# First products on x times its weight ahead of each norm, and four modulation slabs summed beside layer 0's first attention

## The chip, the cores and the metric

One core of a Trainium2 chip runs the whole program. The metric is device time in microseconds, the median of three runs. TensorE multiplies (PE in the profile), VectorE is DVE, ScalarE is ACT, GpSimd is POOL, and SP's queue issues the loads of weights.

## The reference

A first block (RMS norm; three branches: forgetting attention, an S5 state space, memory attention; gated merge; output projection; residual) ends in an outer RMS norm. Two layers follow, on 512 tokens of 1024 features, each modulated by a vector c:

```
ada = silu(c) @ w_ada[l] + b_ada[l]          # shift, scale, gate; twice 3 x 1024
h   = rms(x, g_mix[l]) * (1 + sc1) + sh1
q, k, v of two attentions, gate_a, gate_b = split(h @ w_in[l])
x   = x + gt1 * ((sigmoid(gate_a) * y_a + sigmoid(gate_b) * y_b) @ w_out[l])
h2  = rms(x, g_mlp[l]) * (1 + sc2) + sh2
x   = x + gt2 * (relu(h2 @ w_ff1[l])**2 @ w_ff2[l])
```

`rms(x, g)` divides each token by the root of its mean square and multiplies by g. A product with h can also be made as rstd * (W^T (g (1 + sc) x)) + W^T sh, with rstd one number per token.

## The kernel before

x lies transposed in SBUF, features on partitions, eight blocks k of 128 features by 512 tokens. Each fp32 product is made of three fp32r products: high x high, high x low, low x high. So one tile (128 output features by 512 tokens) is 24 matmuls of 512 columns. Weights come in slabs of 256 columns (1 MB) into a ring of three slots, in one order written by `plan_slabs` (L275); SP issues a slab's load when the slab three before it is used up (`load_weights`, L185). GpSimd splits each slab into a high and a low part, half a slab at a time (L268 high, L272 low), into room for four halves; a half is free when the tile made of it is done. Stages are written out one after another, each engine's queue in program order, with waits on semaphores.

The modulation is 48 slabs, 24 a layer ("ada"). Each is loaded through the same ring, scaled by ScalarE (L395, eight instructions), summed by VectorE (L408), turned by TensorE (L422) and taken by VectorE (L431, L434). `tiles_stage` (L438) does this beside its tiles: scaling and sum two tiles ahead of a slab's last tile, turn and take three tiles later. Four of them lie in the first block's output stage and three in layer 0's.

`norm_stage` (L741) runs four times: at the outer norm and layer 0's mix norm together (`twice`), and at layer 0's MLP norm, layer 1's mix norm and layer 1's MLP norm. Sums of squares are turned by one-column matmuls (L779), then root, reciprocal and spreading transposes (L789); then for each block k VectorE scales (L867), ScalarE adds the shift and rounds (L841), VectorE makes the low part (L860). Matmuls on constants (`warm`, L785) stand in the waits, except in the double norm. Nothing is multiplied by h until h's first block is there.

In a layer the norm is followed by `qkv_stage` (six groups of 96 products), `turn_stage` (transposes), `attention_stage` (16 steps), `wide_attention_stage` (8 steps), mixing, output, the second norm and the MLP. The 16 gate tiles (384 products) are a `Stream` fed between the pieces of the turn and attention stages, by the numbers called paces: 72 by the end of the turn stage, to 252 in the attention stage at 9 a step, to 384 in the wide one at 14 a step. ScalarE takes each stream tile with a Tanh (L2736). The first block's output stage adds x by residue (L2426), squares it twice on ScalarE (L2438, L2440) and adds the squares on VectorE (L2423).

## Time and profile before

| | us |
|---|---|
| median of three runs | 2288.77 (2288.75 to 2291.99) |
| profiled execution | 2291.23 |
| its span | 2289.4 |
| TensorE busy | 2249.8 (98%) |
| GpSimd busy | 1691.9 (74%) |
| VectorE busy | 1259.3 (55%) |
| ScalarE busy | 632.8 (28%) |
| mean granted TensorE clock | 0.992 |

A matmul's record lasts longer than the time to the next one's start, since they are pipelined: read the spacing of starts, not the busy time. The busy time also covers the constants' matmuls and the one-column matmuls in a norm.

### The profile page before, as it was taken

How to read it: one execution, taken by the hardware profiler on the slowest of the kernel's cores; microseconds unless marked ns; L12 is line 12 of the kernel's file. 1: busy time of each engine (PE TensorE's matmuls, PEld its weight loads, DVE VectorE, ACT ScalarE, POOL GpSimd, SP SyncE). 2: the span in 40 equal slices, each digit the busy share in tenths (PEclk: the TensorE clock that was granted, in tenths of full speed). 3: DMA queues.
4: the chain of work that ended last, by engine and by line, in shares of the span. 5: the costliest groups of instructions: out<-in, count | busy, mean ns of one | idle time of the engine just before them, and what ended most of it. 6: DMA issues, size and time to landing. Idle time of an engine off the chain costs nothing.

```text
span 2289.4 us, 31094 instructions
## 1 busy us (share of the span) xinstructions
PE 2249.8 (98%) x11693; PEld 1828.1 (80%) x11693; DVE 1259.3 (55%) x1798; ACT 632.8 (28%) x1286; POOL 1691.9 (74%) x2678
## 2 busy tenths in 40 slices
PE   8999999999999999999999999999999999999999
...
GB/s 204 129 137 153 268 151 35 116 101 159 159 186 186 111 111 94 50 36 39 164 131 189 174 191 177 184 107 97 100 79 33 29 124 92 154 107 107 92 92 56
DMA packets 268656, 280.87 MB, mean 123 GB/s; under 512 B 29964, under 2 KB 240592, under 8 KB 268508
## 3 DMA queue, kind: packets, MB, share of 16 engines
...
## 4 chain that ended last, share of the span: by engine, by line
PE 85%; POOL 6%; DVE 4%; issue 2%; ACT 2%; DMA 1%; SPq 0%; ACTq 0%; DVEq 0%; POOLq 0%
PE ps L496 46%; PE ps L674 14%; PE ps L2527 4%; PE ps L2528 4%; PE ps L2529 4%; POOL ring_low L272 4%; POOL ring_high L268 3%; PE ps L982 2%; PE ps L1025 2%; PE ps L1001 2%; PE ps L1175 1%; PE ps L1182 1%; PE ps L1158 1%; PE ps L2637 1%; DVE ada_acc L408 1%
## 5 line engine op out<-in xcount | busy, mean ns | idle before, releaser
L272 POOL TENSOR_TENSOR ring_low<-ring,ring_high 128x256 fp32r<-128x256 f32 x1309 | 1039.0, 824 | 28.4
L268 POOL TENSOR_SCALAR ring_high<-ring 128x256 fp32r<-128x256 f32 x1309 | 609.1, 491 | 478.3 <-PE ps L674 170.8
L496 PE MATMUL ps<-hT_high,ring_high 128*128 128x512 f32 x704 | 278.0, 395 | 1.4 <-DVE hT_low L860 1.4
L496 PE MATMUL ps<-hT_low,ring_high 128*128 128x512 f32 x704 | 274.9, 390 | 0.0
L496 PE MATMUL ps<-hT_high,ring_low 128*128 128x512 f32 x704 | 274.0, 389 | 0.0
L674 PE MATMUL ps<-hT_high,ring_high 128*128 128x512 f32 x568 | 234.5, 413 | 3.2 <-POOL ring_low L272 1.4
L674 PE MATMUL ps<-hT_high,ring_low 128*128 128x512 f32 x568 | 225.3, 397 | 0.0
L674 PE MATMUL ps<-hT_low,ring_high 128*128 128x512 f32 x568 | 225.1, 396 | 0.0
L408 DVE TENSOR_REDUCE ada_acc<-ring 128x256 f32<-128x2048 f32 x48 | 188.8, 3933 | 54.8 <-ACT ring L395 54.7
L496 PE MATMUL ps<-hidden_high,ring_high 128*128 128x512 f32 x512 | 201.0, 393 | 0.0
L496 PE MATMUL ps<-hidden_low,ring_high 128*128 128x512 f32 x512 | 199.6, 390 | 0.0
L496 PE MATMUL ps<-hidden_high,ring_low 128*128 128x512 f32 x512 | 199.3, 389 | 0.0
L395 ACT ACTIVATE ring<-ring,c_act 128x256 f32<-128x256 f32 x384 | 158.4, 499 | 81.7 <-DMA ring<-in_w_ada_dram 71.4
L2902 DVE SCALAR_TENSOR_TENSOR xT<-ps,ada,xT 128x512 f32<-128x512 f32 x64 | 48.0, 751 | 233.0 <-PE ps L496 233.0
L496 PEld LDWEIGHTS ps<-hT_high,ring_high 128*128 128x128 f32 x704 | 132.1, 188 | 32.1 <-DVE hT_low L860 2.9
L496 PEld LDWEIGHTS ps<-hT_high,ring_low 128*128 128x128 f32 x704 | 132.3, 188 | 28.3
L496 PEld LDWEIGHTS ps<-hT_low,ring_high 128*128 128x128 f32 x704 | 132.3, 188 | 26.0
L2527 PE MATMUL ps<-ring_high,hT_high 128*128 128x512 f32 x384 | 150.6, 392 | 2.1 <-DVE hT_low L860 2.1
L2528 PE MATMUL ps<-ring_high,hT_low 128*128 128x512 f32 x384 | 150.4, 392 | 0.0
L2529 PE MATMUL ps<-ring_low,hT_high 128*128 128x512 f32 x384 | 150.2, 391 | 0.0
L674 PEld LDWEIGHTS ps<-hT_high,ring_high 128*128 128x128 f32 x568 | 106.8, 188 | 40.3 <-issue 17.9
L2943 ACT ACTIVATE relu<-ps 128x512 f32<-128x512 f32 x64 | 38.2, 599 | 347.7 <-PE ps L496 341.8
...
## 6 DMA issues: line engine op xcount, KB each, us to landing
ring<-in_w_in_dram SPq DMA_DIRECT2D x75, 1024.0 KB, 5.3
ring<-in_w_ff_dram SPq DMA_DIRECT2D x64, 1024.0 KB, 5.4
ring<-in_w_ada_dram SPq DMA_DIRECT2D x48, 1024.0 KB, 5.4
ring<-in_w_out_dram SPq DMA_DIRECT2D x12, 1024.0 KB, 5.8
...
ring<-in_w_mem_kv_dram SPq DMA_DIRECT2D x4, 1024.0 KB, 5.4
...
```

The lines of the kernel that those rows point to most:

```text
L268: ins = nc.gpsimd.tensor_scalar(x(hi), x(raw), 1.0, 1.0, ALU.mult, ALU.mult)
L272: ins = nc.gpsimd.tensor_tensor(x(lo), x(raw), x(hi).bitcast(F32), ALU.subtract)
L395: ins = K.nc.scalar.activation(w[:, k, :], w[:, k, :], ACT.Copy, scale=K.c_act[:, k:k + 1])
L408: K.nc.vector.tensor_reduce(K.ada_acc[:, n % 2, :], K.slot(slab).rearrange("p k n -> p n k"), AX_X, ALU.add).then_inc(K.sig("ada_scaled"). ...
L496: return nc.tensor.matmul(out[0:rows, bank, cols[0]:cols[1]], lhsT, rhs, start=start, stop=stop)
L674: ins = K.nc.tensor.matmul(out, lhsT, rhs, start=start, stop=stop)
L982: ins = nc.tensor.matmul(s_view(i, u, w)[:, c:c + n], lhsT, rhs, start=True, stop=st["diagonal"] is None or c + n < w)
L1001: ins = nc.tensor.transpose(t_view(u, w)[:, b * P:(b + 1) * P], probs[j % P_BUFS][:, u, b * P:(b + 1) * P], K.ident)
L2527: nc.tensor.matmul(out, xh, hi[:, y, :], start=k == 0, stop=False)
L2528: nc.tensor.matmul(out, xl, hi[:, y, :], start=False, stop=False)
L2529: ins = nc.tensor.matmul(out, xh, lo[:, y, :], start=False, stop=k == KD - 1)
L2902: return v.scalar_tensor_tensor(K.xT[:, m, :], ps[:, 0, :], gate[:, m:m + 1], K.xT[:, m, :], ALU.mult, ALU.add)
```

## The change

The two first gate tiles of each layer, and the first hidden tile of each MLP, are made on x times its weight g(1 + sc), without the root. Their two operands (high by ScalarE, low by VectorE) are made during the eight tiles ahead of the norm. In the norm, TensorE goes through the eight blocks k: the tiles' products, then two two-column matmuls a tile that multiply the shift by the same weights, with the turning and spreading of the root between blocks. VectorE scales the finished tiles by the root; the shift's product goes in as a bias of the Tanh or Relu. The normed h is written over the same two operands, each block after its products are done (`used`). The gate slab `m{l}0ga` so moves ahead of the qkv slabs. The stream has 14 tiles (336 products) with new paces. In the first norm of all and the MLP norms the scaled block lies in PSUM instead of SBUF.

One modulation slab leaves the first block's output stage and three leave layer 0's output stage: four are now done beside layer 0's first attention, a third of a slab's scaling and a third of its sum per step. The mixing stage no longer waits for the last stream tile before its fourth tile, and the first sums of squares in the first output stage move from ahead of the tile's addition into `ahead`.

```diff
     for i in range(4):
         add("out", T["w_out"][0], dm, 0, D, part=i)
-        ada(0)
+        if i < 3:
+            ada(0)
...
+        add(f"m{l}0ga", w2, dm, 3072, D, part=0)
...
         for mp in range(4):
-            add(f"m{l}{mp}ga", w2, dm, 3072, D, part=mp)
+            if mp:
+                add(f"m{l}{mp}ga", w2, dm, 3072, D, part=mp)
+                if l == 0 and mp > 1:
+                    ada(0)
             add(f"m{l}{mp}gb", w2, dm, 4096, D, part=mp)
+            if l == 0 and mp in (1, 2):
+                ada(0)
...
-            if l == 0 and i < 3:
-                ada(0)
...
+    def scale(self, e, i):
+        K = self.K
+        slab, r = self.due(i)
+        if slab is None:
+            return
+        if r == 0:
+            K.slab_here(e, slab)
+        w = K.slot(slab)
+        for k in range(3 * r, min(3 * r + 3, KD)):
+            ins = K.nc.scalar.activation(w[:, k, :], w[:, k, :], ACT.Copy, scale=K.c_act[:, k:k + 1])
+        if r == 2:
+            ins.then_inc(K.sig("ada_products").sem, 1)
+    def add(self, e, i):
+        K = self.K
+        slab, r = self.due(i - 3)
+        if slab is None:
+            return
+        l, x = K.ada_slab[slab]
+        n = l * 24 + x
+        if r == 0:
+            e.wait_ge(K.sig("ada_products").sem, n + 1)
+            e.wait_ge(K.sig("ada_summed").sem, n - 1)
+        cols = ((0, 86), (86, 171), (171, 256))[r]
+        ins = K.nc.vector.tensor_reduce(K.ada_acc[:, n % 2, cols[0]:cols[1]],
+                                        K.slot(slab)[:, :, cols[0]:cols[1]].rearrange("p k n -> p n k"), AX_X, ALU.add)
+        if r == 2:
+            ins.then_inc(K.sig("ada_scaled").sem, 1)
+    def sum(self, pe, j):
+        K = self.K
+        slab, r = self.due(j - 5)
+        if slab is None or r:
+            return
+        l, x = K.ada_slab[slab]
+        n = l * 24 + x
+        pe.wait_ge(K.sig("ada_scaled").sem, n + 1)
+        pe.wait_ge(K.sig("ada_taken").sem, n)
+        for c in range(2):
+            ins = K.nc.tensor.transpose(K.ps[:, 4, SLAB_W + c * P:SLAB_W + (c + 1) * P],
+                                        K.ada_acc[:, n % 2, c * P:(c + 1) * P], K.ident)
+        ins.then_inc(K.sig("ada_summed").sem, 1)
+    def take(self, e, j):
+        K = self.K
+        slab, r = self.due(j - 5)
+        if slab is None or r:
+            return
+        l, x = K.ada_slab[slab]
+        n = l * 24 + x
+        e.wait_ge(K.sig("ada_summed").sem, n + 1)
+        K.link(e, "dve_step", K.nc.vector.tensor_reduce(
+            K.ada_col[:, n % 2, :], K.ps[:, 4, SLAB_W:2 * SLAB_W].rearrange("p (c k) -> p c k", c=2), AX_X, ALU.add))
+        K.nc.vector.tensor_tensor(K.ada[:, l, 2 * x:2 * x + 2], K.ada_col[:, n % 2, :], K.b_ada[l][:, 2 * x:2 * x + 2], ALU.add
+                                  ).then_inc(K.sig("ada_taken").sem, 1)
 def tiles_stage(K, tiles, banks, act=None, dve=None, act_on=None, after=None, entry=None, arriving=None, tensor_entry=None, act_lead=4,
-                also=None, ahead=None, ada_bank=7, late=None, entry_at=None, waits=None, ada_lead=2, ada_lag=3, back=None):
+                also=None, ahead=None, ada_bank=7, late=None, entry_at=None, waits=None, ada_lead=2, ada_lag=3, back=None, done=0):
...
+                first = 2 + done
                 size = len(tiles[0])
...
-def norm_stage(K, src, gain, dst, shift, sums, last, twice=None, banks=(7, 6, 1)):
+def factors_ahead(K, e, shift):
...
+        self.high, self.low = K.sig("unnormed_high"), K.sig("unnormed_low")
+        self.base = self.high.total
+        self.high.total += KD
+        self.low.total += KD
+    def round_up(self, e, k):
+        K = self.K
+        K.nc.scalar.activation(K.hT[0][:, k, :], self.src[:, k, :], ACT.Copy, scale=self.gain[:, k:k + 1]
+                               ).then_inc(self.high.sem, 1)
+    def low_part(self, e, k):
+        K = self.K
+        e.wait_ge(self.high.sem, self.base + k + 1)
+        K.nc.vector.scalar_tensor_tensor(K.hT[1][:, k, :], self.src[:, k, :], self.gain[:, k:k + 1],
+                                         K.hT[0][:, k, :].bitcast(F32), ALU.mult, ALU.subtract).then_inc(self.low.sem, 1)
+def norm_stage(K, src, gain, dst, shift, sums, last, unnormed, tiles, places, made, take, twice=None):
...
+                pe.wait_ge(unnormed.low.sem, unnormed.base + k + 1)
+                for n, t in enumerate(tiles):
+                    if k == 0:
+                        K.weight_here(pe, t[0][5])
+                    for x in range(3 * k, 3 * k + 3):
+                        _, rows, cols, lhsT, rhs, _, start, stop = t[x]
+                        ins = nc.tensor.matmul(ps[0:rows, tile_banks[n], cols[0]:cols[1]], lhsT, rhs, start=start, stop=stop)
+                ins.then_inc(used.sem, 1)
+            def shift_of(n, k):
+                for x in (3 * k, 3 * k + 2):
+                    ins = nc.tensor.matmul(ps[:, shift_bank, 2 * n:2 * n + 2], tiles[n][x][3], K.shift_two[:, k, :],
+                                           start=x == 0, stop=x == 3 * KD - 1)
+                if (n, k) == (len(tiles) - 1, KD - 1):
+                    ins.then_inc(made.sem, len(tiles))
...
+            def turn(bank, parts):
+                for t in range(TT):
+                    for n, x in enumerate(parts):
+                        ins = nc.tensor.matmul(ps[:, bank, t:t + 1], x[:, t * P:(t + 1) * P], K.ones[:, 0:1],
+                                               start=n == 0, stop=n == len(parts) - 1)
+                ins.then_inc(turned.sem, 1)
...
+            pe.wait_ge(taken.sem, taken.total - 2)
+            for k in range(KD):
+                products_of(k)
+                if twice is not None:
+                    squared, summed = twice[0]
+                    for h in (2 * k, 2 * k + 1):
+                        shift_of(h // KD, h % KD)
+                    if k == 1:
+                        pe.wait_ge(taken.sem, taken.total)
+                        pe.wait_ge(summed.sem, summed.total)
+                        pe.wait_ge(squared.sem, squared.total - 1)
+                        turn(turn_bank, (sums, last))
+                    if k == 3:
+                        pe.wait_ge(inverted.sem, i0 + 1)
+                        spread_root(root_bank, 4)
+                    if k == 4:
+                        pe.wait_ge(squared.sem, squared.total)
+                        turn(other_bank, (twice[3], twice[4]))
+                    if k == 6:
+                        pe.wait_ge(inverted.sem, i0 + 2)
+                        spread_root(other_bank, 1)
+                else:
+                    for h in range(len(tiles) * k, len(tiles) * (k + 1)):
+                        shift_of(h // KD, h % KD)
+                    if k == (2 if len(tiles) == 1 else 1):
+                        pe.wait_ge(taken.sem, taken.total)
+                        turn(turn_bank, (sums, last))
+                    if k == (4 if len(tiles) == 1 else 2):
+                        pe.wait_ge(inverted.sem, i0 + 1)
+                        spread_root(root_bank, 4)
...
+                pe.wait_ge(copied.sem, c0 + 1)
...
+            unnormed.round_up(e, KD - 1)
...
-                nc.scalar.activation(dst[0][:, k, :], tmp[:, k % 2, :], ACT.Identity, bias=shift[:, k:k + 1]
+                e.wait_ge(used.sem, u0 + k + 1)
+                nc.scalar.activation(dst[0][:, k, :], tmp[k % 2], ACT.Identity, bias=shift[:, k:k + 1]
...
+                if k == 0 and twice is not None:
+                    e.wait_ge(root.sem, o0 + 2)
+                    v.reciprocal(nar[:, 1, :], nar[:, 0, :]).then_inc(inverted.sem, 1)
                 if k >= 1:
                     low_part(k - 1)
             low_part(KD - 1)
+            K.link(e, "dve_step", v.tensor_copy(rstd[:, :], ps[:, root_bank, :]))
+            e.wait_ge(made.sem, made0 + len(tiles))
+            for n in range(len(tiles)):
+                K.link(e, "dve_step", v.tensor_reduce(K.shift_of[:, n:n + 1], ps[:, shift_bank, 2 * n:2 * n + 2], AX_X, ALU.add))
+                take(e, n, ps[:, tile_banks[n], :], rstd[:, :])
...
+                    if beside is not None and len(beside) > 2:
+                        beside[2](pe, j)
...
-    tmp = R("normed0", [P, 2, SEQ], 57344)
+    tmp = [ps[:, b, :] for b in (0, 3)]
...
-                if k >= 2:
-                    e.wait_ge(by_act.sem, by_scalar.index(k) + 1)
-                v.scalar_tensor_tensor(tmp[:, k % 2, :], K.xT[:, k, :], K.g_norm[:, k:k + 1], ps[:, 1, :], ALU.mult,
+                if k >= 1:
+                    e.wait_ge(by_act.sem, by_scalar.index(max(k, 3)) + 1)
+                v.scalar_tensor_tensor(tmp[k % 2], K.xT[:, k, :], K.g_norm[:, k:k + 1], ps[:, 1, :], ALU.mult,
...
+        if n < KD - 1:
+            unnormed.round_up(e, n)
...
+    def first_gains(e, n):
+        if n == 0:
+            mix_gains(K, e, 0)
+        if n >= 2:
...
+        if n >= 1:
+            unnormed.low_part(e, n - 1)
...
-    summed.total += KD - 3
...
+    summed.total += KD - 2
...
+                if g == 1:
+                    pe.wait_ge(*gates_scaled)
...
+            e.wait_ge(*gates_turned)
...
+    K.link(e, "gains_ready", x)
+    factors_ahead(K, e, ada[:, 0:8])
...
+    def scale_gates(e, n, ps, rstd):
+        v.tensor_tensor(scaled_gates[n][:, :], ps, rstd, ALU.mult)
+        v.tensor_scalar(K.half_shift[:, n:n + 1], K.shift_of[:, n:n + 1], 0.5, None, ALU.mult).then_inc(gates_scaled.sem, 1)
...
+            if mp or b == "b":
+                tiles += column_tiles(K, K.first[f"m{l}{mp}g{b}"], 2, KD, K.hT)
...
+    def turn_gates(e):
+        e.wait_ge(gates_scaled.sem, gates_scaled.total)
+        for n in range(2):
+            nc.scalar.activation(gates[n], scaled_gates[n][:, :], ACT.Tanh, scale=0.5, bias=K.half_shift[:, n:n + 1]
+                                 ).then_inc(gates_turned.sem, 1)
...
+    if l == 0:
+        slabs = GateSlabsBeside(K, [i for i in sorted(K.ada_slab) if K.first["m00gb"] < i < K.first["m00p"]])
+        beside = (slabs.scale, slabs.add, slabs.sum, slabs.take)
...
-                    [72 + 9 * i for i in range(18)] + [240, 252])
+                    [72] + [85 + 8 * i for i in range(17)] + [220, 226], beside=beside)
...
-                         [(252, 252, 274)] + [(278 + 14 * i, 284 + 14 * i, 288 + 14 * i) for i in range(7)] + [(376, 382, 384)])
+                         [(226, 226, 246)] + [(249 + 10 * i, 254 + 10 * i, 256 + 10 * i + 8 * (i == 6)) for i in range(7)] + [(328, 334, 336)])
...
-    tiles_stage(K, tiles, 2, dve=mix_dve, also=mix_high, waits={(0, 0): (al.sem, al0 + 4), (0, 12): (yl.sem, yl0 + 2)})
+    tiles_stage(K, tiles, 2, dve=mix_dve, also=mix_high, tensor_entry={x: y for x, y in before.items() if x != "stream"},
+                entry_at=(3, {"stream": before["stream"]}), waits={(0, 0): (al.sem, al0 + 4), (0, 12): (yl.sem, yl0 + 2)})
...
-        if n == KD - 1:
+        if n == 0:
             if l == 0:
                 taken = K.sig("ada_taken")
                 e.wait_ge(taken.sem, 20)
-            v.scalar_tensor_tensor(gains[:, 1, :], ada[:, 32:40], 1.0, K.g_mlp[l], ALU.add, ALU.mult).then_inc(ga.sem, 1)
-    tiles_stage(K, column_tiles(K, K.first[f"out{l}"], KD, KD, split), 1, dve=out_dve, ahead=mlp_gain,
+            K.link(e, "gains_ready", v.scalar_tensor_tensor(gains[:, 1, :], ada[:, 32:40], 1.0, K.g_mlp[l], ALU.add, ALU.mult))
+            factors_ahead(K, e, ada[:, 24:32])
+        else:
+            unnormed.low_part(e, n - 1)
+    def out_high(e, n):
+        if n < KD - 1:
+            e.wait_ge(added.sem, added0 + n + 1)
+            unnormed.round_up(e, n)
+    tiles_stage(K, column_tiles(K, K.first[f"out{l}"], KD, KD, split), 1, dve=out_dve, also=out_high, ahead=mlp_gain,
                 arriving=(xl, xl0, before, 5))
...
+    def scale_first(e, n, ps, rstd):
+        v.tensor_tensor(rel[:, n, :], ps, rstd, ALU.mult).then_inc(first_scaled.sem, 1)
...
+    arriving = norm_stage(K, K.xT, gains[:, 1, :], K.hT, ada[:, 24:32], K.sums, K.square_last, unnormed,
+                          column_tiles(K, K.first[f"ff1{l}00"], 1, KD, K.hT), ((0,), 4, 7, 5, None, (3, 6)), K.sig("tile_made"),
+                          scale_first)
+    first_scaled.total += 1
...
+    after[5] = 0
...
+        if n == 0:
+            e.wait_ge(first_scaled.sem, scaled0 + 1)
+            return nc.scalar.activation(rel[:, 0, :], rel[:, 0, :], ACT.Relu, bias=K.shift_of[:, 0:1])
...
-        if l + 1 < LAYERS and n == len(tiles) - 2:
+        if l + 1 < LAYERS and n == last_eight:
             mix_gains(K, e, l + 1)
+        elif l + 1 < LAYERS and n > last_eight:
+            K.unnormed.low_part(e, n - 1 - last_eight)
+    def next_high(e, n):
+        if l + 1 < LAYERS and last_eight <= n < len(tiles) - 1:
+            e.wait_ge(added.sem, hidden0 + n + 1)
+            K.unnormed.round_up(e, n - last_eight)
...
-                arriving=arriving, ada_bank=7 if back is None else 6, back=back)
+                also=next_high, done=1, arriving=arriving, ada_bank=7 if back is None else 6, back=back)
```

## Rows read from the trace of the kernel before

**Rows 1.** The page: busy us, share of the span, instructions of each engine.
```profile
PE 2249.8 (98%) x11693; PEld 1828.1 (80%) x11693; DVE 1259.3 (55%) x1798; ACT 632.8 (28%) x1286; POOL 1691.9 (74%) x2678
```

**Rows 2.** Timeline about norms and output stage: start us, us, engine, line, shape.
```profile
741.62 0.39 PE L496 MATMUL ps<-merged_high,ring_low 128*128 128x512 f32 x1
...
757.06 0.77 PE L2527 MATMUL ps<-ring_high,hT_high 128*128 128x512 f32 x1 [1.59 <-DVE hT_low L860]
...
1135.12 0.50 PE L496 MATMUL ps<-mixed_high,ring_high 128*128 128x512 f32 x1 [2.16 <-POOL ring_low L272]
...
1157.36 0.40 PE L496 MATMUL ps<-mixed_high,ring_low 128*128 128x512 f32 x1
...
1164.68 0.47 PE L496 MATMUL ps<-hT_high,ring_high 128*128 128x512 f32 x1 [0.64 <-DVE hT_low L860]
...
1521.04 0.40 PE L496 MATMUL ps<-hidden_high,ring_low 128*128 128x512 f32 x1
...
1527.93 0.47 PE L2527 MATMUL ps<-ring_high,hT_high 128*128 128x512 f32 x1 [0.54 <-DVE hT_low L860]
...
1922.87 0.40 PE L496 MATMUL ps<-mixed_high,ring_low 128*128 128x512 f32 x1
...
1931.46 0.47 PE L496 MATMUL ps<-hT_high,ring_high 128*128 128x512 f32 x1 [0.57 <-DVE hT_low L860]
```

**Rows 3.** Windows: stretch, length, busy us of each engine, granted clock, DMA.
```profile
745.00:757.00 12.00, 10.47 (x48) 9.90 (x48) 2.56 (x6) 2.65 (x7) 7.28 (x13) 0.50 0.53 174
757.00:762.00 5.00, 4.94 (x12) 3.95 (x13) 4.89 (x8) 2.44 (x4) 0.00 (x0) 0.50 0.01 2
694.70:700.60 5.90, 5.90 (x14) 4.64 (x15) 1.05 (x3) 0.36 (x1) 5.82 (x12) 0.50 0.78 265
```

**Rows 4.** Chain of waits: start us, us; products, then two attention steps.
```profile
1846.85 76.43 PE ps L496 x336
...
939.26 2.27 PE ps L674 x9
...
944.49 2.28 PE ps L674 x9
```

**Rows 5.** Timeline: one-column matmuls, VectorE in the first output stage.
```profile
743.49 0.95 PE L779 MATMUL ps<-const,squares_summed 128*128 128x1 f32 x8
...
713.18 3.97 DVE L408 TENSOR_REDUCE ada_acc<-ring 128x256 f32<-128x2048 f32 x1 [3.22 <-ACT ring L395]
...
721.26 1.84 DVE L2423 TENSOR_TENSOR squares_summed<-squares_summed,square 128x512 f32<-128x512 f32 x2 [1.38 <-ACT square L2440]
...
743.02 1.09 DVE L2426 SCALAR_TENSOR_TENSOR x_by_residue<-ps,xT 128x512 f32<-128x512 f32 x1
```

**Rows 6.** Lines: count, busy us, mean ns of one, idle before.
```profile
L860 DVE SCALAR_TENSOR_TENSOR hT_low<-normed,ada,hT_high 128x512 fp32r<-128x512 f32 x32 | 27.5, 861 | 0.9
L2000 DVE TENSOR_TENSOR hT_low<-normed,hT_high 128x512 fp32r<-128x512 f32 x8 | 7.7, 968 | 0.0
L395 ACT ACTIVATE ring<-ring,c_act 128x256 f32<-128x256 f32 x384 | 158.4, 499 | 81.7 <-DMA ring<-in_w_ada_dram 71.4
```

**Rows 7.** Waits of TensorE: total us, times, longest us.
```profile
PE ps L1175 <- DVE probs_b L1221: 3.2, 3, 1.5
PE ps L496 <- ACT gates L2736: 2.1, 2, 1.1
PE ps L982 <- ACT probs_a L1046: 1.2, 2, 0.6
```

**Rows 8.** Timeline of GpSimd: layer 0's output stage, then its qkv stage.
```profile
1129.79 1.51 POOL L268 TENSOR_SCALAR ring_high<-ring 128x256 fp32r<-128x256 f32 x4 [9.20 <-DMA ring<-in_w_out_dram]
...
765.30 3.04 POOL L268 TENSOR_SCALAR ring_high<-ring 128x256 fp32r<-128x256 f32 x4 [12.86 <-PE ps L2529]
...
871.74 1.51 POOL L268 TENSOR_SCALAR ring_high<-ring 128x256 fp32r<-128x256 f32 x4
```

**Rows 9.** DMA issue in 707 to 717 us: KB, us to landing.
```profile
ring<-in_w_ada_dram SPq DMA_DIRECT2D x1, 1024.0 KB, 7.9
```

184 lines of the change are left out of this document (95 added, 89 removed).

## The prediction

> **What bounds the kernel now.** I read the page's first part, then TensorE's waits, then the timeline, product by product, about each stretch that the change touches. TensorE is busy 98% of the span [rows 1], and the chain of waits runs down one long row of it: 336 products take 76.43 us, 0.2275 each [rows 4]. All other engines have idle time, so the kernel gets faster only where TensorE's starts lie further apart than that. The change leaves the number of large products as it is. What it can win is idle time ahead of norms and at joints, and it pays with small matmuls.
>
> The four norms are such stretches. Between the last product of one stage and the first of the next, less that product's own 0.2275, lie 15.2 us in the double norm (741.62 to 757.06), 7.1 in layer 0's MLP norm, 6.7 in layer 1's mix norm and 8.4 in layer 1's MLP norm [rows 2]. The first is dearer still: the granted clock stands at 0.50, the lower level (1.2 GHz), from 745 to 762, where TensorE has 48 small records in 12 us, and from 757 to 762 only 12 products start where 22 would at 2.4 GHz [rows 3]. That is another 2.3 us, so this norm costs 17.5.
>
> **The price of the small matmuls.** A record of 8 one-column matmuls lasts 0.95 us, so one takes 0.12 [rows 5]; in it each matmul of the code stands twice, so four turns with two parts each are 16, 1.9 us. The change puts 16 two-column matmuls into a norm for each tile made ahead: a column more, so I take 0.11 each (bounds 0.06, half of that, if they overlap better between large ones, and 0.2275, a product of 512 columns; below nothing is excluded, since they are added). A switch back to large products I price at 0.09 a block, the lateness of a first product behind small ones; its bounds are 0 and 0.37. The first product at 1135.12, after an idle stretch, has a record 0.1 longer than the 0.40 of the others, and the one at 757.06, at the lower clock, 0.37 longer [rows 2]. A double-tile block thus costs 24 products a 4 blocks as before plus 4 x 0.11 + 0.09.
>
> **Layer 0's MLP norm and layer 1's.** One tile, 24 products (5.5 us) move into the norm from behind it. Eight blocks with two small ones each cost 8 x (0.22 + 0.09) = 2.5, the turn 1.9, the spreading about 0.5: 4.9 us of overhead where 7.1 and 8.4 were idle. Gains 2.1 and 3.4. The root must be there by the time that TensorE is through: VectorE's first two normed blocks follow at once.
>
> **Layer 1's mix norm.** Two tiles, 48 products. Overhead 8 x (0.44 + 0.09) + 1.9 + 0.5 = 6.6, idle 6.7: nothing, 0.
>
> **The double norm.** Two tiles and two turns: overhead 4.2 + 3.8 + 1, 9 us against 17.5. But here the chain of VectorE decides. In the first block's output stage each tile gives it x by residue 1.09, a wait of 1.38 for ScalarE's square, two sums 1.84 and now a low part, about 0.86: 5.17 in a tile of 24 x 0.2275 = 5.46 [rows 5, 6], and two to three slabs' sums of 3.97 come between. It goes into the norm some 5 us late instead of level with TensorE. I place the finished squares at 750: the last residue began at 743.02 [rows 5] and starts up to 5 us later now. TensorE, which has 12 products and 8 small ones to do (k = 0 and 1, to 748), waits there 2 us or so for its first turn. From there the root, 7 blocks and the scaling bring the first qkv product to about 766.5, with 48 products (10.9 us) done before it: 759.4 + 10.9 - 766.5, some 3.8 us gained. A stop of 3 us has cost the clock before: after 691 to 694.6, only 14 products start in 5.9 us at 0.50, where 26 would, so 2.7 are lost [rows 3]. At a chance of 4 in 10, with some for further lateness, I take +2 (range -1 to +7).
>
> **Output stages.** The stream of loads loses three slabs ahead of layer 0's MLP. GpSimd there sat 9.20 us waiting for w_out's weights [rows 8] behind a modulation slab, and TensorE 2.16 us for GpSimd [rows 2]. That goes: +2.2, or 0 if the load is late for another reason.
>
> **Stream and joints.** The stream loses 48 products in each layer; a step of attention, 5.23 us with 9 products [rows 4], becomes 5.0 with 8. TensorE has no gap in it, so this is time that went to the norm, no more. Waits at joints now get products or are moved: the first attention step's 1.2, the last wide step's 3.2, and the mix stage's 2.1 for the last Tanh [rows 7]. All that is 6.5; I take 6. Its bounds are 0 and 6.5. In the wide steps 10 products instead of 14 shield VectorE's chain, which shortens the step by 0.9 us; if that chain then ends last, 0.5 a step in 14 steps would be lost, 7.
>
> **Four slabs beside attention.** A step of 5 us takes three scalings, 3 x 158.4 / 384 = 1.24 us of ScalarE, and a third of a sum, 3.97 / 3 = 1.32 of VectorE [rows 5, 6]. Both have room. The slabs' places in the ring do not: each slot is free only after its sum, three steps after it began. The third slab's load is issued behind another and takes 7.9 us to land [rows 9], while the step that wants it comes 5 to 7 us later. ScalarE then stands 3 us ahead of exponentials, of which it has some 2 us in hand. I take -2 for the two late slabs (range 0 to -6).
>
> **Load stage.** The scaled block moves to PSUM, so the low part reads SBUF once. It takes 0.97 now, against 0.86 for the norms' [rows 6], which do more. VectorE is the limit there; with 0.15 to 0.2 less over 7 blocks I take +1.3 (0 to 2).
> The Trainium skill, "SBUF — State Buffer", "Who interferes with whom", says that a VectorE instruction with two SBUF inputs contends with a GpSimd instruction that reads SBUF, and that one with a single such input doesn't. [Rows 6] agree in that the instruction beside GpSimd's work is the longer one. The same rule speaks against the change elsewhere: the new low parts take both inputs from SBUF, eight ahead of each norm, while GpSimd splits weights.
>
> **GpSimd in the qkv stages.** Its room is four halves. The gate slab's halves are used in the norm, but not free before it ends, and fill two of the four: at the qkv stage's start the reserve is two halves instead of four. Layer 0's stage shows it running 20 halves back to back, (871.74 - 765.30) / 19 = 5.60 us a half [rows 8], against TensorE's 5.46. It had two halves in hand and I find one and a half microseconds left of it, after 11.2 lost and what the earlier start (no wait of 12.86 us into the stage, [rows 8]) gives back. Expected loss 1.5 for both layers together, bounds 0 and 10 a layer.
>
> **The sum.** 2.1 + 3.4 + 0 + 2 + 2.2 + 6 - 2 + 1.3 - 1.5 = 13.5, less nothing for the two low parts' contention, since GpSimd in the output stages has 0.3 us a half over. The profiled execution is 2291.23: 2277.7 after. It lies 2.46 above the median of the runs (2288.77), so the median comes to 2275.
>
> **Rivals.** First, *all idle time fills*: the small matmuls cost 0.06 (96 of them, 4.8 us less), slabs and GpSimd hold nobody (3.5), the double norm gives 2 more. Gain 24, time 2265. For it: TensorE's small records overlap everywhere; against: the 0.95 for eight. Second, *the reserve is just short and the double norm stays late*: -4 in each layer from GpSimd instead of 1.5 in both, 0 instead of 2 in the norm; gain 13.5 - 6.5 - 2 = 5, time 2283.8. For it: 5.60 against 5.46. Third, on the other side, *GpSimd becomes the bound of both qkv stages*. It decides from 5.75 us a half; the first half after 765.30 shows 3.04 for its high part alone, twice the 1.51 of others [rows 8], because VectorE works beside it. At 6.2 a half on average, 22 halves lose 22 x 0.74 - 5.6 = 10.7 in each layer, 21 in all. The sum without its own 1.5 is 15: 2288.8 - 15 + 21 = 2295. Fourth, *the change doesn't do what it says*: the slabs beside attention hold ScalarE, and TensorE behind it, 1 us in each of 12 steps: 12 lost instead of 2, time 2285, about the same as before.
>
> **Numbers.** Chances: forecast 0.60, all fills 0.17, just short 0.11, slabs 0.04, GpSimd bound 0.08. A measurement of this kernel can tell 0.2%, 4.6 us: faster means under 2284.2, slower over 2293.3. Faster then holds the forecast, the first rival and a part of the second, 0.80; same 0.12; slower 0.08. The range for 8 in 10 is 2265 to 2287: sum of the bounds of the norm (-3, +5), slabs (-4, +2) and GpSimd (-10, +1.5).
>
> **What would show it.** In the norms the products of the first tiles, spaced 0.2275, with small matmuls of 0.11 between; first qkv product near 766 and a granted clock of 1 there, or a stop at 748 if VectorE is late. No wait of TensorE for Tanh, for probs_b or probs_a at the joints; none of GpSimd for w_out. Attention steps of 5.0 in layer 0 and 1 alike: longer ones in layer 0 mean the slabs. Waits of TensorE for ring_low within qkv would show GpSimd as the bound, and a steady one of more than 3 us a group would make the prediction wrong.

## The result and the profile after

The changed kernel takes 2279.33 us in the median of five runs (2273.96 to 2281.3), the kernel before 2289.27 (2288.75 to 2291.99). The ratio is 0.9948, with an interval of 0.9935 to 0.996: faster by 0.5%, 10 us, where 2275 and a range of 2265 to 2287 were predicted. The profiled execution after is the quickest of the five (2273.96, span 2272.2), the one before was the upper end of its runs (2291.23). The two profiles so lie 17.3 us apart, more than the medians do. For that reason the changed kernel was run and profiled once more, as the first experiment. That run is called "again" (2278.97 in the median, span 2277.1 in its profile), and both profiles are read here. "The changed kernel" stands for the first of them, the quicker one.

The page's first line after, columns as in [rows 1]:

```profile
PE 2239.9 (99%) x11743; PEld 1829.0 (80%) x11743; DVE 1306.1 (57%) x1868; ACT 653.1 (29%) x1317; POOL 1707.1 (75%) x2678
```

The timeline of TensorE after, about the double norm, answers to [rows 2]:

```profile
739.38 0.39 PE L576 MATMUL ps<-merged_high,ring_low 128*128 128x512 f32 x1
...
740.06 0.39 PE L903 MATMUL ps<-hT_high,ring_low 128*128 128x512 f32 x1
743.42 0.50 PE L903 MATMUL ps<-hT_high,ring_high 128*128 128x512 f32 x1 [2.97 <-POOL ring_low L272]
743.75 0.39 PE L903 MATMUL ps<-hT_low,ring_high 128*128 128x512 f32 x1
743.98 0.40 PE L903 MATMUL ps<-hT_high,ring_low 128*128 128x512 f32 x1
744.22 0.17 PE L909 MATMUL ps<-shift_two,ring_high 128*128 128x2 f32 x1
...
744.47 0.25 PE L909 MATMUL ps<-shift_two,ring_low 128*128 128x2 f32 x1
744.58 0.66 PE L903 MATMUL ps<-hT_high,ring_high 128*128 128x512 f32 x1
...
764.95 0.48 PE L2682 MATMUL ps<-ring_high,hT_high 128*128 128x512 f32 x1
```

The products of the two tiles begin 0.22 us after the output stage's last one. The first qkv product comes at 764.95 with 48 products already done, which is 10.9 us of the stream's work: before it came at 757.06 with none, and 2.3 us of half clock behind it. From the output stage's last product (739.38, before 741.62) to the first qkv product it is 25.57 us, of which 10.92 are the 48 products: 14.65. Before it was 15.44, and 2.3 more for the half clock. So the norm is 3.1 us shorter by this count. The four small matmuls take 0.36 us by their starts (744.22 to 744.58).

The same view of the second profile, "again":

```profile
721.18 0.39 PE L576 MATMUL ps<-merged_high,ring_low 128*128 128x512 f32 x1
725.25 0.66 PE L428 MATMUL ps<-const,ada_acc 128*128 128x128 f32 x2 [3.68 <-DVE ada L440]
...
744.30 0.39 PE L576 MATMUL ps<-merged_high,ring_low 128*128 128x512 f32 x1
...
747.98 0.25 PE L909 MATMUL ps<-shift_two,ring_low 128*128 128x2 f32 x1
751.08 0.56 PE L917 MATMUL ps<-const,squares_summed 128*128 128x1 f32 x2 [2.85 <-ACT square L2579]
...
771.12 0.48 PE L2682 MATMUL ps<-ring_high,hT_high 128*128 128x512 f32 x1
```

Here TensorE stops twice for the chain of squares and sums: at 721, where it wants to turn a modulation slab that VectorE has not taken, and at 748, before the first turn. The qkv stage starts 6.2 us later than in the other profile. The windows tell the clock's part in it: stretch, length, busy us of each engine, granted clock. First the changed kernel, then "again":

```profile
720.00:765.00 45.00, 40.12 (x201) 33.72 (x199) 28.79 (x36) 14.94 (x28) 31.59 (x48) 0.92 0.36 117
```

```profile
720.00:771.00 51.00, 44.48 (x202) 37.57 (x202) 33.03 (x37) 16.59 (x32) 34.26 (x51) 0.83 0.33 106
```

A mean of 0.83 over 51 us says that a third of the stretch ran at 1.2 GHz, 0.92 over 45 us that it was a sixth.

The other three norms go nearly as forecast. Ahead of layer 0's MLP norm the output stage's last product is at 1148.54, and the next stage begins at 1159.76 with 24 products (5.5 us) in between. Less one spacing, that leaves 5.5 us of overhead where 7.1 were idle before and 4.9 was forecast, with the clock at 0.90 (window below, in the experiments). In layer 1's MLP norm the overhead is 4.0. The rows of layer 0's:

```profile
1148.54 0.39 PE L576 MATMUL ps<-mixed_high,ring_low 128*128 128x512 f32 x1
1149.44 0.17 PE L909 MATMUL ps<-shift_two,ring_high 128*128 128x2 f32 x1
1149.47 0.25 PE L909 MATMUL ps<-shift_two,ring_low 128*128 128x2 f32 x1
1149.58 0.48 PE L903 MATMUL ps<-hT_high,ring_high 128*128 128x512 f32 x1
1149.90 0.40 PE L903 MATMUL ps<-hT_low,ring_high 128*128 128x512 f32 x1
...
1159.76 0.48 PE L576 MATMUL ps<-hT_high,ring_high 128*128 128x512 f32 x1
```

By their starts the two small matmuls of a block take 0.14 us, and the first product behind them 0.32 instead of 0.2275.

The waits of TensorE after (total us, times, longest), which answer to [rows 7]:

```profile
PE ps L903 <- POOL ring_low L272: 3.0, 1, 3.0
PE ps L428 <- DVE ada L440: 1.9, 1, 1.9
PE ps L1125 <- ACT probs_a L1191: 1.6, 2, 1.2
...
PE ps L1322 <- DVE probs_b L1368: 0.4, 2, 0.2
```

The last wide step's wait (3.2) and the mix stage's (2.1) are gone. The one for probs_a stands in another place: not in the first step of attention, but behind a modulation slab.

### The profile page after: what moved, and what is told of

It is laid out like the page before. It is cut to its first block, busy times and chain, and to the rows that moved or that the text cites. A ratio compares the mean times of both kernels' runs of the same rounds, so it can differ in the third digit from the quotient of the medians.

```text
span 2272.2 us, 31339 instructions
## 1 busy us (share of the span) xinstructions
PE 2239.9 (99%) x11743; PEld 1829.0 (80%) x11743; DVE 1306.1 (57%) x1868; ACT 653.1 (29%) x1317; POOL 1707.1 (75%) x2678
## 4 chain that ended last, share of the span: by engine, by line
PE 83%; POOL 8%; DVE 3%; DMA 2%; ACT 2%; issue 2%; SPq 1%; ACTq 1%; DVEq 0%; POOLq 0%
PE ps L576 45%; PE ps L756 13%; POOL ring_low L272 4%; PE ps L2682 4%; PE ps L2683 4%; PE ps L2684 4%; POOL ring_high L268 3%; PE ps L1125 2%; PE ps L1170 2%; PE ps L1144 2%; PE ps L903 2%; PE ps L1329 1%; PE ps L1322 1%; PE ps L1305 1%; DMA ring<-in_w_in_dram 1%
## 5 line engine op out<-in xcount | busy, mean ns | idle before, releaser
L272 POOL TENSOR_TENSOR ring_low<-ring,ring_high 128x256 fp32r<-128x256 f32 x1309 | 1054.5, 836 | 28.3
L576 PE MATMUL ps<-hT_high,ring_high 128*128 128x512 f32 x688 | 271.3, 394 | 0.8 <-POOL ring_low L272 0.8
L576 PE MATMUL ps<-hT_low,ring_high 128*128 128x512 f32 x688 | 268.6, 390 | 0.0
L576 PE MATMUL ps<-hT_high,ring_low 128*128 128x512 f32 x688 | 267.7, 389 | 0.0
L756 PE MATMUL ps<-hT_high,ring_high 128*128 128x512 f32 x536 | 218.9, 408 | 2.3 <-POOL ring_low L247 1.4
L756 PE MATMUL ps<-hT_low,ring_high 128*128 128x512 f32 x536 | 214.2, 400 | 0.0
L756 PE MATMUL ps<-hT_high,ring_low 128*128 128x512 f32 x536 | 213.5, 398 | 0.0
L414 DVE TENSOR_REDUCE ada_acc<-ring 128x256 f32<-128x2048 f32 x44 | 173.0, 3932 | 37.8 <-ACT ring L401 37.7
L401 ACT ACTIVATE ring<-ring,c_act 128x256 f32<-128x256 f32 x352 | 145.3, 499 | 72.6 <-DMA ring<-in_w_ada_dram 64.0
L576 PEld LDWEIGHTS ps<-hT_high,ring_high 128*128 128x128 f32 x688 | 129.1, 188 | 28.4 <-DVE hidden_low L3169 1.2
L756 PEld LDWEIGHTS ps<-hT_high,ring_high 128*128 128x128 f32 x536 | 100.8, 188 | 28.8 <-issue 7.9
```

The source lines that it names most:

```text
L272: ins = nc.gpsimd.tensor_tensor(x(lo), x(raw), x(hi).bitcast(F32), ALU.subtract)
L401: ins = K.nc.scalar.activation(w[:, k, :], w[:, k, :], ACT.Copy, scale=K.c_act[:, k:k + 1])
L414: K.nc.vector.tensor_reduce(K.ada_acc[:, n % 2, :], K.slot(slab).rearrange("p k n -> p n k"), AX_X, ALU.add).then_inc(K.sig("ada_scaled"). ...
L576: return nc.tensor.matmul(out[0:rows, bank, cols[0]:cols[1]], lhsT, rhs, start=start, stop=stop)
L756: ins = K.nc.tensor.matmul(out, lhsT, rhs, start=start, stop=stop)
```

## The experiments

In most expectations two readings of the case stand against each other, theory A and rival B; each experiment says which one the run bears out. No run takes one part of the change out alone, but for the load stage's block and the mix stage's wait: what the first tiles and the moved slabs are worth is read from the profiles before and after.

**The changed kernel again.** No edit.

> The changed kernel once more. Its five times lie in two groups, 2274 (twice) and 2279 to 2281 (three times); the profile of it is of one at 2274. Theory A: the groups differ by the granted clock about the double norm, where TensorE stops twice (2.1 us at 720, 3.1 us at 740) for VectorE and GpSimd; then an execution near 2280 shows more time at the lower level there, and one at 2274 the same as before. Rival B: the groups come from the order in which loads land, and the granted clock is the same in both while another wait of TensorE is longer by 5 us. Both expect 2274 to 2281 again, about 0.995 of the kernel before.

2278.97 us (2278.26 to 2281.53), ratio 0.9953. The two profiles differ by 4.9 us of span. From the first product of the first output stage (687 and 689 us) to the first qkv product they part by 4.1 us. Another 1.5 part them between 196 and 235 us, where the stretch at the lower clock lasts 6.8 us instead of 3.4, and 1.6 come back in layer 1's mix norm in the same way. Theory A holds: most of it is the stops about the double norm, and the clock after them. VectorE's timeline shows where the two part. The same steps, first in the changed kernel, then in "again":

```profile
735.91 1.88 DVE L2594 TENSOR_TENSOR squares_summed<-squares_summed,square 128x512 f32<-128x512 f32 x2 [1.31 <-ACT square L2581]
737.71 0.88 DVE L852 SCALAR_TENSOR_TENSOR hT_low<-x_by_residue,gains,hT_high 128x512 fp32r<-128x512 f32 x1
738.52 1.07 DVE L2567 SCALAR_TENSOR_TENSOR x_by_residue<-ps,xT 128x512 f32<-128x512 f32 x1
```

```profile
734.59 2.30 DVE L2594 TENSOR_TENSOR squares_summed<-squares_summed,square 128x512 f32<-128x512 f32 x2 [0.57 <-ACT square L2581]
736.82 1.22 DVE L852 SCALAR_TENSOR_TENSOR hT_low<-x_by_residue,gains,hT_high 128x512 fp32r<-128x512 f32 x1
737.96 1.08 DVE L2567 SCALAR_TENSOR_TENSOR x_by_residue<-ps,xT 128x512 f32<-128x512 f32 x1
740.36 2.28 DVE L2594 TENSOR_TENSOR squares_summed<-squares_summed,square 128x512 f32<-128x512 f32 x2 [1.31 <-ACT square L2581]
```

The same instructions take 1.88 and 0.88 us in one execution, 2.30 and 1.22 in the other. A tile (734.59 to 740.36) is then 5.77 us, over TensorE's 5.46, and VectorE falls behind with each. A tile at the shorter durations (735.91 to 740.89) is 5.0. Measured from the stage's first product, VectorE is at the same place in both at 710 us and 2.4 us later in "again" at 740. What sends an execution into the one or the other is not shown.

A tile also holds 1.31 us in which VectorE stands idle for ScalarE's squares of the block it has just made. A low part of the block before, put ahead of that wait, would lie in it, and by these rows the tile would be about 4.6 us (an estimate; no run tries it).

**Low parts with a single SBUF input.** The low part of x times its weight is left out: a sum over one element, a copy of the high part, stands in its place.

```diff
-        K.nc.vector.scalar_tensor_tensor(K.hT[1][:, k, :], self.src[:, k, :], self.gain[:, k:k + 1],
-                                         K.hT[0][:, k, :].bitcast(F32), ALU.mult, ALU.subtract).then_inc(self.low.sem, 1)
+        with K.nc.allow_low_precision(reason="one input"):
+            K.nc.vector.tensor_reduce(K.hT[1][:, k, :], K.hT[0][:, k, :].bitcast(F32).unsqueeze(2), AX_X, ALU.add
+                                      ).then_inc(self.low.sem, 1)
```

> The unnormed low parts (32 in all, eight ahead of each norm) are made by an instruction with a single SBUF input, a sum over one element of the high part; so the low part of x times its weight is wrong, and nothing else changes. Theory A (the low parts with two SBUF inputs hold GpSimd up): a half of a slab falls from about 6.2 us to 5.2 in the first output stage, GpSimd is level with TensorE at 740, the wait of 3.0 us for ring_low at the double norm's start goes, and the time falls by 3 us (2 to 6). Rival B (GpSimd is late for its loads, or because of the other VectorE work): halves stay over 5.8 us and the wait stays over 2 us, the time moves by less than 1 us.

2276.84 us (2271.45 to 2279.21), ratio 0.994 (0.9927 to 0.9952): 2.1 us under "again", inside the spread of either. Of GpSimd's halves that begin between 709 and 743.5 us one takes 5.1 us on average, from the start of its high part to the end of its low part, as in the kernel before; in the two profiles of the changed kernel it took 5.5 and 5.6. The three that begin between 725 and 739 us take 5.3, where they took 6.0 and 5.8. No wait for ring_low is left at the norm. So the new low parts do slow GpSimd. But TensorE waited 3.2 us for the squares instead. Theory A names one of two things that are late there, and the other is left.

The Trainium skill, "SBUF — State Buffer", "Who interferes with whom", says that a VectorE instruction with two SBUF inputs contends with a GpSimd instruction that reads SBUF. The trace agrees in direction: 5.5 or 5.6 us a half with two inputs, 5.1 with one.

**Low parts in the norm.** Two low parts ahead of each norm, the other six at its start:

```diff
+AHEAD = 2
...
-            unnormed.low_part(e, KD - 1)
+            for k in range(AHEAD, KD):
+                unnormed.low_part(e, k)
...
-        if n >= 1:
+        if 1 <= n <= AHEAD:
             unnormed.low_part(e, n - 1)
...
-        else:
+        elif n <= AHEAD:
             unnormed.low_part(e, n - 1)
...
-        elif l + 1 < LAYERS and n > last_eight:
+        elif l + 1 < LAYERS and last_eight < n <= last_eight + AHEAD:
             K.unnormed.low_part(e, n - 1 - last_eight)
```

> Two of eight low parts are made ahead of each norm, six at its start, where VectorE waits for the root; nothing is left out. Theory A (GpSimd is slowed by the low parts): the gate slab's second half is ready 2 to 3 us earlier at the double norm, the wait for ring_low falls below 1 us, and TensorE takes the low parts as they come (0.9 us each against 1.8 a block); time -2 us (-4 to 0). Rival B (VectorE is the late one there): six low parts push the root's reciprocal and the normed blocks back, the norms lengthen by 1 to 2 us each, and the time rises by 2 to 6 us.

2279.19 us (2277.75 to 2284.14), as "again" in the median. The profile shows that one gain and two losses cancel. From the first output stage's first product to the first qkv product it gains 3.5 us on the quicker profile of the changed kernel and 7.6 on "again"; layer 0's MLP norm loses 3.0 and layer 1's 4.3. Neither theory holds whole: the wait for ring_low is 1.7 us and not under 1, and it is the MLP norms alone that lengthen, by more than rival B's 1 to 2 us. In those, one tile's block takes TensorE 0.9 us and a low part takes VectorE about as long (0.86 in [rows 6]). TensorE waits 2.5 us for low parts in all, and the clock is lower. The window of layer 0's MLP norm, changed kernel first:

```profile
1148.00:1165.00 17.00, 17.00 (x88) 14.67 (x87) 11.15 (x16) 5.63 (x10) 16.18 (x28) 0.90 0.39 124
```

```profile
1148.00:1165.00 17.00, 15.76 (x73) 13.60 (x72) 13.83 (x19) 4.42 (x8) 14.06 (x20) 0.80 0.37 119
```

**The same in the double norm alone.**

```diff
-            unnormed.low_part(e, KD - 1)
+            for k in range(KD - 1 if twice is None else 2, KD):
+                unnormed.low_part(e, k)
...
-        if n >= 1:
+        if 1 <= n <= 2:
             unnormed.low_part(e, n - 1)
```

> As lows_in_norm, but in the double norm alone: two low parts ahead, six at its start; the other three norms are as in the changed kernel. Nothing is left out. In the profile of lows_in_norm the double norm ends 8.7 us earlier than in the one of again, while the MLP norms lose 3.0 and 4.6 us. Theory A (VectorE's tile in the first output stage, 5.7 us with the low part in again, is what is late there, and moving low parts out of it brings it under TensorE's 5.46): the first turn waits less than 0.5 us, no time at the lower level from 740 to 755, and the time is 2271 to 2274, 5 to 8 us under again. Rival B (the 8.7 are two draws of the same spread): 2276 to 2281 as again.

2270.67 us (2267.84 to 2272.21), ratio 0.9915 (0.9901 to 0.9928), 8.3 us under again's median: all its runs lie under all of the changed kernel's. The ratios to the kernel before, each taken beside it, are 0.9915 and 0.9953 with intervals that don't touch. Theory A holds. VectorE's timeline in it:

```profile
740.59 2.30 DVE L2595 TENSOR_TENSOR squares_summed<-squares_summed,square 128x512 f32<-128x512 f32 x2 [0.58 <-ACT square L2582]
742.82 1.05 DVE L2568 SCALAR_TENSOR_TENSOR x_by_residue<-ps,xT 128x512 f32<-128x512 f32 x1
743.97 5.09 DVE L852 SCALAR_TENSOR_TENSOR hT_low<-x_by_residue,gains,hT_high 128x512 fp32r<-128x512 f32 x6
```

The last block's product with the residue begins at 742.82, where it began at 749.12 in "again", and the six low parts lie where VectorE stood idle. No wait for the squares is left, only one of 1.9 us for GpSimd's low parts at the norm's start. The granted clock is 1.00 from 740 to 755 us, and 0.96 over this window:

```profile
720.00:765.00 45.00, 40.54 (x210) 34.09 (x209) 30.92 (x38) 17.68 (x33) 35.40 (x53) 0.96 0.39 125
```

The profiles of the other runs bear this out. From the first output stage's first product to the first qkv product the six whose code is the same there take 76.2 to 82.0 us; the four with six low parts moved (lows_in_norm, lows_double and the two of the last experiment) take 72.7 to 74.8. With a single SBUF input it is 79.1, inside the first group: less contention alone didn't do it in the one profile of it.

**Fewer shift matmuls.** Most of the shift's product is left out:

```diff
                 for x in (3 * k, 3 * k + 2):
+                    if x not in (0, 3 * KD - 1):
+                        continue
```

> Of the 96 two-column matmuls in the norms only the first and the last of each tile are left (12), so the shift's product is wrong; 84 are gone. In the changed kernel's trace four of them take 0.09 each by their starts and the products around them lose 0.1 more a block. Theory A (the norms are bound by TensorE): the four norms shorten by 84 x 0.09 plus 0.1 to 0.2 for most of 28 blocks, 8 to 11 us in all. Rival B (in the norms the chain root, reciprocal, spreading, two normed blocks bounds, or GpSimd does): the starts in the norm move closer, but a wait for the root or for hT_low takes their place, and less than 5 us is gained.

2268.46 us (2265.71 to 2271.53), ratio 0.9908: 10.5 us under again. By marks in the profiles the four norms are 7.5 us shorter than in "again" (1.5, 2.1, 3.2, 0.7), just under what theory A expected; the rest lies elsewhere, 2.0 of it in the slabs' attention, which no edit touched (the next experiment shows why). Layer 1's mix norm is the clean one: no wait, and a granted clock of 1.00 in both profiles. There 28 small matmuls and six whole switches are gone, which at 0.09 and 0.1 is 3.1 us, and 3.2 are gained. In the double norm a wait of 4.5 us for the squares took part of the gain, as rival B has it, and the 0.7 of the last norm lies within what profiles of the same code differ by there (1.6 us).

**Slabs later.** The four slabs beside attention begin at other steps:

```diff
-        a, r = divmod(step, 3)
-        return (self.slabs[a], r) if 0 <= a < len(self.slabs) else (None, r)
+        for a, start in enumerate((0, 3, 7, 10)):
+            if start <= step < start + 3:
+                return self.slabs[a], step - start
+        return None, 1
```

> Beside layer 0's first attention the four slabs begin at steps 0, 3, 7 and 10 instead of 0, 3, 6 and 9. Nothing is left out. Theory A (ScalarE stands 3.6 and 2.9 us for the third and fourth slab's load, and TensorE loses 1.5 to 2 us behind it): the first wait goes or falls below 1 us, the second too, the two long steps (6.5 and 5.7 us) fall to 5.1 and 1 to 1.5 us are gained, which the times can hardly tell: the steps' spacing in the profile decides. Rival B (the steps are long because of the transposes and the takes, not the load): three steps stay above 5.5.

2273.8 us (2267.56 to 2276.18), ratio 0.9926 (0.9911 to 0.9941). In the changed kernel ScalarE and TensorE show the late load (timelines of ScalarE, then of TensorE):

```profile
956.75 1.31 ACT L467 ACTIVATE ring<-ring,c_act 128x256 f32<-128x256 f32 x3 [3.64 <-DMA ring<-in_w_ada_dram]
...
972.48 1.31 ACT L467 ACTIVATE ring<-ring,c_act 128x256 f32<-128x256 f32 x3 [2.85 <-DMA ring<-in_w_ada_dram]
```

```profile
952.93 1.13 PE L1125 MATMUL ps<-ak,aq 64*128 64x256 f32 x8
...
959.44 0.92 PE L1125 MATMUL ps<-ak,aq 64*128 64x256 f32 x6 [1.22 <-ACT probs_a L1191]
```

A step of 5.0 us has become one of 6.5. With the slabs later, both waits for the load are gone, and no step is longer than 5.2:

```profile
947.68 1.13 PE L1127 MATMUL ps<-ak,aq 64*128 64x256 f32 x8
...
952.68 1.14 PE L1127 MATMUL ps<-ak,aq 64*128 64x256 f32 x8
...
957.69 1.13 PE L1127 MATMUL ps<-ak,aq 64*128 64x256 f32 x8
```

From the first attention step to the last it is 74.7 us, 2.1 less than the 76.8 in "again". The median gains 5, more than this explains. What the rest comes of is not shown; the stretch about the double norm, where profiles of the same code differ by up to 5.8 us, can hold it. So the steps decide, for theory A.

The run with fewer shift matmuls shows how much lateness ScalarE hides. Its attention has the slabs at the old steps and takes 74.8 us. The load is late there too, but less:

```profile
957.50 1.31 ACT L467 ACTIVATE ring<-ring,c_act 128x256 f32<-128x256 f32 x3 [2.06 <-DMA ring<-in_w_ada_dram]
```

Waits of 2.06 and 2.42 us lengthen their steps to 5.2 and 5.3 us, while 3.64 makes 6.5 and 2.85 makes 5.7. So ScalarE has some 2 us in hand, as the prediction said, and the later steps are worth 0.1 to 2.1 us, by when the load lands.

**Mix stage waits for the Tanh again.**

```diff
-    tiles_stage(K, tiles, 2, dve=mix_dve, also=mix_high, tensor_entry={x: y for x, y in before.items() if x != "stream"},
-                entry_at=(3, {"stream": before["stream"]}), waits={(0, 0): (al.sem, al0 + 4), (0, 12): (yl.sem, yl0 + 2)})
+    tiles_stage(K, tiles, 2, dve=mix_dve, also=mix_high, waits={(0, 0): (al.sem, al0 + 4), (0, 12): (yl.sem, yl0 + 2)})
```

> TensorE waits again for the last Tanh of the stream ahead of the mixing stage, as in the kernel before. Theory A (a gain of 1 us a layer by that move): each mixing stage starts 0.8 to 1.2 us later in the profile, with a wait for ScalarE's gates, and 2 us are lost in both. Rival B (the Tanh is hidden anyway, since VectorE's chain ends last there): less than 0.5 us lost in both.

2278.54 us (2277.26 to 2278.83), no different from "again" in the median. In the profile the wait is back:

```profile
PE ps L576 <- ACT gates L2908: 2.0, 2, 1.0
```

Only 0.58 and 0.61 us of it reach the end of the mixing stages, by the first products of the output stages (1105 and 1866 us in the changed kernel), since the changed kernel has a gap of 0.4 us early in the same stages. A loss of 1.2 us in both together lies between the theories.

**The load stage's block in SBUF, and in PSUM in the kernel before.**

```diff
-    tmp = [ps[:, b, :] for b in (0, 3)]
+    in_sbuf = R("normed0", [P, 2, SEQ], 57344)
+    tmp = [in_sbuf[:, b, :] for b in range(2)]
```

The run of the kernel before makes the opposite edit, with the wait for ScalarE that the banks need:

```diff
-    tmp = R("normed0", [P, 2, SEQ], 57344)
+    tmp = [ps[:, b, :] for b in (0, 3)]
...
-                if k >= 2:
-                    e.wait_ge(by_act.sem, by_scalar.index(k) + 1)
+                if k >= 1:
+                    e.wait_ge(by_act.sem, by_scalar.index(max(k, 3)) + 1)
```

> In the load stage the scaled block lies in SBUF again, so the low part has two SBUF inputs. Theory A: the low part takes 0.97 us instead of 0.75 to 0.8, GpSimd's first high parts 0.7 instead of 0.5, and TensorE gets its eighth block 1.2 to 1.5 us later in the profile. Rival B (the gain at the start comes of the earlier takes, not of the place): the eighth block is less than 0.3 us later.

> The kernel before with one part of the change alone: the load stage's scaled block lies in PSUM. Theory A (the place shortens the low part, 0.93 to 0.68 us, and VectorE's chain bounds there): the sixteenth of the first products starts 10.3 us after the first instead of 11.6, and 1 to 1.5 us are gained. Rival B (in sbuf_block the sixteenth came after 10.4 us with the block in SBUF, so the 11.6 of the kernel before were an accident of phase with GpSimd): less than 0.5 us gained in the median. The times can hardly tell 1 us; the low part's duration and the spacing decide.

> The kernel of sbuf_block once more, for a second profile of it. Theory A expects the low part at 0.81 to 0.97 us and the sixteenth product 10.4 to 11.7 us after the first, with more than 1 us lost against again in one of the two profiles. Rival B expects 10.4 again.

With the block in SBUF the changed kernel takes 2280.72 us (2278.66 to 2283.09), and 2272.95 in the single execution of its second profile. The kernel before with PSUM takes 2286.66 (2285.57 to 2289.67), 2.7 us less than without the edit in the medians, ratio 0.999 (0.9981 to 1.0): an interval from no gain to 4 us, too wide to decide about 1 us. From TensorE's first high x high product to its sixteenth it is 10.3 us in all 11 profiles with the block in PSUM (the edited kernel before among these), and 11.6 (the kernel before), 10.4 and 10.9 us in the three with it in SBUF. So the part is worth 0.1 to 1.3 us. In the kernel before theory A holds, with 10.3 instead of 11.6; in the changed kernel the two profiles with SBUF lose 0.1 and 0.6, less than its 1 us. The rows show VectorE and GpSimd slowing each other in two different pairings. First VectorE in the kernel before with the block in PSUM; then both engines in the kernel before as it was, and in the second profile of the SBUF kernel:

```profile
16.55 0.68 DVE L2000 TENSOR_TENSOR hT_low<-ps,hT_high 128x512 fp32r<-128x512 f32 x1
```

```profile
16.86 0.84 POOL L241 TENSOR_SCALAR ring_high<-ring 128x256 fp32r<-128x256 f32 x1
...
18.14 0.93 DVE L2000 TENSOR_TENSOR hT_low<-normed,hT_high 128x512 fp32r<-128x512 f32 x1
```

```profile
15.44 1.04 POOL L247 TENSOR_TENSOR ring_low<-ring,ring_high 128x256 fp32r<-128x256 f32 x1
16.45 0.40 POOL L241 TENSOR_SCALAR ring_high<-ring 128x256 fp32r<-128x256 f32 x1
...
18.09 0.81 DVE L2148 TENSOR_TENSOR hT_low<-normed,hT_high 128x512 fp32r<-128x512 f32 x1
```

In PSUM VectorE's low part takes 0.68 us, and GpSimd's high and low parts 0.40 and 0.73. In the SBUF kernel they take 0.81, 0.40 and 1.04; in the kernel before 0.93, 0.84 and 0.73. What decides between the two pairings is not shown.

**Both edits that gained: the best version.** lows_double and slabs_later together, and then with the turn of modulation slabs one tile later in the first output stage:

```diff
-                arriving=(added, merged0 + 16, {}, 6))
+                arriving=(added, merged0 + 16, {}, 6), ada_lag=4)
```

> lows_double and slabs_later together; nothing is left out. The first gained 8.3 us against again in its median, the second 2.05 us between two marks of the attention stage in its profile. Theory A (they touch different stages and add): 2268 to 2270, 0.9905 of the kernel before or lower. Rival B (what the attention stage gives back is lost again in layer 0's mixing or output stage, which wait for the weights of GpSimd): 2270 to 2273, as lows_double.

> As best, and in the first output stage a modulation slab is turned four tiles after it was due instead of three. Theory A (TensorE's stop of 2.7 to 3.8 us at about 721 stands for VectorE's take of the slab before, which lies behind a 4 us sum, and one tile more of distance covers 5.46 us of it): the stop falls below 0.5 us and 2 to 3 us are gained on best. Rival B (VectorE is behind by as much in any case, since its tiles with a slab take over 8 us): the stop moves to the next slab's turn or to the first turn of sums, and less than 1 us is gained.

Both together take 2267.96 us (2264.05 to 2270.62), ratio 0.9908 (0.9894 to 0.9923) to the kernel before. "Again" had 0.9953, so this one is some 10 us under the changed kernel, and 20 under the kernel before. lows_double alone had 0.9915, and the intervals overlap: that the two add is seen in the profile, for theory A, not in the times. The attention stage takes 74.7 us there against 76.6 in lows_double's profile, and the 1.9 us stay to layer 0's output stage. With the later turn it is 2269.03 (2268.11 to 2269.69): the stop at 721 is gone, and one of 4.5 us stands at 727 (TensorE's waits):

```profile
PE ps L428 <- DVE ada L440: 4.5, 1, 4.5
```

That is rival B: VectorE is what is late, and the turn's place does not change that. The best version keeps the three tiles.

## Why the prediction was right, and where it was not

The forecast was a gain of 13.5 us from a median of 2288.77. The medians differ by 10 us (ratio 0.9948), and the measured 2279.33 lies 4 us above the forecast 2275. By the marks that both kernels share, from before's profile to "again", the one near the median, the steps gave:

| step | forecast | measured |
|---|---|---|
| load stage | +1.3 | +1.2 |
| rest of the first block | 0 | +0.2 |
| first output stage, with its slabs | 0 | -4.0 |
| double norm | +2 | +1.8 |
| GpSimd's reserve in two qkv stages | -1.5 | 0 |
| four slabs beside attention | -2 | -2.8 |
| joints, both layers | +6 | +5.7 |
| layer 0's output stage | +2.2 | +3.2 |
| layer 0's MLP norm | +2.1 | +1.9 |
| layer 1's mix norm | 0 | +0.8 |
| layer 1's MLP norm | +3.4 | +4.3 |
| sum | 13.5 | 12.3 |

In the quicker profile the output stage is at -1.2, the double norm at +3.1 and the load stage with the first block at +3.4, but layer 1's mix norm, with 3.4 us at the lower clock in it, at -0.7. With 17.3 us its distance to the kernel before is also that of a high draw of the one to a low draw of the other. The spans put "again" 12.3 us below before's profile; the medians are 10 apart because that profile was itself 2 us above its median.

The terms that carry the gain (joints, layer 0's output stage, the MLP norms) came out for the reasons given. That the sum came out so near is in part luck: 4.0 us lost in the output stage, where 0 was written, and 1.6 more in five smaller differences, stand against 4.4 us above the forecast, in GpSimd's reserve, layer 0's output stage and both norms of layer 1 above all. The range has a slip too. The bounds that it names add up to 2266.5 to 2292, not 2265 to 2287; the measurement lies in both.

**The double norm.** The forecast said that VectorE's chain decides, that it comes in late and that TensorE waits at 748 for the squares, and put the first qkv product at 766.5. It came at 764.95 and at 771.12. "Again" has the wait in that place (2.85 us at 748), and lows_double, which moves six low parts out of the output stage, shows that it was this chain: 8.3 us. The size was off. 5.17 us a tile was summed from rows in which VectorE worked without low parts; with them the sums take 2.30 instead of 1.84 and the low part 1.22 instead of 0.86, and the tile is 5.77. The loss fell in the output stage, where 0 had been written: from its first product to its last it takes 55.2 us in "again", with the stop of 3.7 us at 721, against 51.1 before and 51.4 in lows_double.

**GpSimd and the low parts.** "Less nothing, since GpSimd has 0.3 us a half over" failed as a step. Low parts with two SBUF inputs slow GpSimd (5.5 to 5.6 us a half, 5.1 with one input and in the kernel before), and the quicker execution stops 2.97 us for it at 740. There GpSimd is the late one and VectorE is not. What was set against the change and then costed at nothing was worth up to 3 us in that execution; in "again" VectorE's own instructions were the longer ones.

**GpSimd's reserve in qkv.** Priced at 1.5 us and at 21 as a rival; nothing was lost. In layer 0's stage GpSimd waits once, at the start, and TensorE waits for it in neither layer's:

```profile
765.28 1.95 POOL L268 TENSOR_SCALAR ring_high<-ring 128x256 fp32r<-128x256 f32 x4 [12.27 <-PE ps L909]
...
877.75 1.51 POOL L268 TENSOR_SCALAR ring_high<-ring 128x256 fp32r<-128x256 f32 x4
```

The rate was read rightly: between these rows lie 20 halves, 5.62 us each, where 5.60 was read. The reserve was not. Against TensorE's 5.46 a half they fall behind by 3.2 us in all, less than one of the two halves in hand; 11.2 had been written off.

From the first qkv product to the first attention product it is 154.7 us after, and 157.1 before with 2.3 us of half clock in it, for the same 648 large products.

**Slabs beside attention.** The load of the third slab was forecast to hold ScalarE 3 us, with -2 in all. It held it 3.64, and the fourth 2.85; with the slabs at later steps 2.1 of the 2.8 came back.

**Small matmuls.** They were taken at 0.11 with 0.09 a switch. Four of them take 0.36 and two 0.14, and the first product behind them 0.32 instead of 0.2275: 0.09 or 0.07 each, and 0.1. That lies between the forecast's 0.11 and the rival's 0.06. No row stood behind the 0.5 for the spreading; it takes 0.40.

**Joints.** Of the mix stage's part four tenths were covered by something else: with the wait put back 1.2 us were lost and not 2.1. The rest of the joints was right, since the last wide step has no wait over 0.2 left.

**Layer 1's norms.** 0 and 3.4 gave 0.8 and 4.3. Of the nine profiles with the same code in the mix norm six take 17.0 us and three 18.5, against 17.8 before (6.9 and the 48 products); the granted clock from there to the qkv stage is 1.00 in "again" and 0.91 in the first profile. So the step is +0.8 or -0.7. Before's profile had 3.4 us at the lower clock inside the last norm, and no row here separates that from the change.
